# Last half chunk of an MLP by seven block products, with the last products and the final gains moved

## The chip, the cores and the metric

One Trainium2 chip, one of its cores. The metric is the device time of one execution in microseconds (us).

## The reference

A decoder block on x (256 rows, 1024 columns, float32): two attention paths, gated and added (all of it before the part that is changed), then

```
h2 = rmsnorm(x, g_mlp)
u = relu(h2 @ w_ff1)                  # 256 x 4096
x = x + (u * u) @ w_ff2               # 4096 x 1024
return rmsnorm(x, g_final)
```

## The kernel before

**Tiling.** The 4096 columns of u go in 8 chunks of 512 (`FAST` = 7 is the last), each in two halves p of 256. Every float32 operand is split into a high part, a copy in the fp32r type by ScalarE (`high_...`), and a low part, the difference by VectorE (`low_...`). `product` (L1453) multiplies by three matmuls: high by high, high by low, low by high.

For a half chunk TensorE computes u transposed (`mlp_in`, L1794: 48 matmuls of 256 columns into bank 4), ScalarE applies relu and squares it (`relu_square`, L864). The half's share of the output is then a product of 256 x 256 by 256 x 1024, taken as 2 x 2 blocks: rows 0 to 127 and 128 to 255, columns 0 to 511 and 512 to 1023 (C11, C12, C21, C22).

**Seven or eight products.** Taken plainly this is eight block products, each of three matmuls of 512 columns. For chunks 1 to 6 `mlp_products` (L1845) does seven (Winograd's form of Strassen's method), of sums of blocks: `left_sums` (VectorE) and `lefts_high`/`lefts_low` for the left side; on the right T1 and T3 by accumulating DMAs of GpSimd (`sum_blocks`, L522, on top of an extra load of SyncE into `t3_raw`, L424) and T2 and T4 by VectorE (`block_sums`). The seven results stay in seven PSUM banks and are accumulated over chunks 1 to 6.

**The end.** Chunk 7 is done plainly in both halves. TensorE's order is: the products of (6,0), `mlp_in` of (7,0), the seven products of (6,1), `mlp_in` of (7,1), then eight calls of `mlp_out_last` (L1816) of two block products each, in the order below. The last call makes C22 in two quarters of 256 columns.

```
mlp_out_last(0, 0, 0); mlp_out_last(0, 0, 1); mlp_out_last(1, 0, 0)      # t, p, n
mlp_out_last(0, 1, 0); mlp_out_last(0, 1, 1); mlp_out_last(1, 0, 1)
mlp_out_last(1, 1, 0); mlp_out_last(1, 1, 1)
```

While `mlp_in` of (7,1) runs, VectorE adds the seven banks into `xs`, the rows of x (`combine_banks`, L1324; later `combine_rows`), which also frees four of them for the plain products.

**The final norm.** As each C block is ready (`ff_done`), VectorE adds it to `xs` (`residual`, L1209, which gives `fin_res`) and, for rows 0 to 127, multiplies by the final gains (`gain`, L1411, which gives `fin_gain`). ScalarE sums the squares of the first rows (L586). VectorE adds the two sums (L1424, `fin_sum`), GpSimd takes the power -1/2 (L549, `fin_rstd`), and ScalarE scales. ScalarE's order is fixed: squares of C11 and C12, `final_act(0, 0)` (waits for `fin_gain` 1 and `fin_rstd` 1), squares of the two quarters of C22 (`ff_done` 4 and 5), `final_act(0, 1)`, `final_act(1, 0)`. For the last rows GpSimd adds the last sum (L553) and takes the power (L556); VectorE scales the quarters (L1446) and they are stored.

**Queues.** SyncE issues the weight loads in program order, each after a wait for its slot of four; ScalarE, VectorE, GpSimd and TensorE also run strictly in program order.

Of the kernel before, what the change touches and what calls it, by code (L numbers as in the profile page):

```python
# [13 lines left out]
P = 128  # L14
# [89 lines left out]
PRODUCTS = ((P1, A11, B11), (P4, A22, T4), (P7, S3, T3), (P5, S1, T1), (P2, A12, B21), (P6, S2, T2), (P3, S4, B22))  # L104
FAST = FF_CHUNKS - 1
# [13 lines left out]
def hybrid_block(nc, x, g_mix, w_in, b_gate, g_cq, w_q_up, g_ckv, w_kv_up, w_o_a, w_o_b, w_out,  # L119
# [10 lines left out]
    with ExitStack() as ctx:  # L130
# [63 lines left out]
        tail_bank = ps[:, U_BANK, P:P + QUART]  # L194
# [106 lines left out]
        last_part = sem("last_part")  # L301
# [80 lines left out]
        def _(sp):  # L382
# [33 lines left out]
            def load_w2(c, p):  # L416
# [6 lines left out]
                if 1 <= c < FAST:  # L423
                    sp.dma_start(t3_raw[:, p, :], w2_rows(c, p)[:, 0, HALF:D]).then_inc(t3_landed[p], 16)  # L424
# [27 lines left out]
            load_w2(FAST, 1)  # L452
# [14 lines left out]
        def _(pool):  # L467
# [96 lines left out]
        def _(act):  # L564
# [311 lines left out]
            def u_high(p):  # L876
                act.wait_ge(u_sq, FAST * 2 + p + 1)
                act.wait_ge(w2_used, FAST * 2 + p - 1)
                copy(left_hi_of[p][:, HALF:], left_raw[p][:, HALF:]).then_inc(uT_hi_done, 1)

            def mlp_chunk(c, first=False, last=False):
# [12 lines left out]
                if last:  # L894
                    high_last(0)
                    relu_square(c + 1, 0)
                else:
                    high_blocks(c + 1, 0)
                    high_t24(c + 1, 0)
                    relu_square(c + 1, 0)  # L900
                    high_t3(c + 1, 0)
# [53 lines left out]
        def _(dve):  # L955
# [249 lines left out]
            def residual(i, done, ready):  # L1205
# [3 lines left out]
                nc.vector.tensor_tensor(xr, ps[:, ROW_BANK[i], :], xr, ALU.add).then_inc(ready, 1)  # L1209
# [74 lines left out]
            def low_last(p):  # L1284
                s, w = (U_FF + 2 + p) % SLOTS, SLOT_W // 2
                for h in range(2):
                    dve.wait_ge(last_hi, 2 * p + h + 1)
                    nc.vector.tensor_tensor(wlo[:, s, h * w:(h + 1) * w], raw[:, s, h * w:(h + 1) * w],
                                            whi[:, s, h * w:(h + 1) * w].bitcast(F32),
                                            ALU.subtract).then_inc(last_lo, 1)  # L1290

            def left_sums(c, p):
# [9 lines left out]
                nc.vector.tensor_tensor(r[:, S4, :], r[:, S2, :], r[:, A12, :], ALU.subtract).then_inc(s_part, 1)  # L1302
# [653 lines left out]
```

## Time and profile before

| what | us |
|---|---|
| median of 3 runs (360.7 to 361.22) | 360.95 |
| the profiled execution | 361.16 |
| its span in the profile | 359.4 |
| TensorE busy | 353.2 (98%) |
| VectorE busy | 286.0 (80%) |
| ScalarE busy | 229.2 (64%) |
| GpSimd busy | 39.7 (11%) |

The profiled execution took 1.76 us more than its span. The busy time of TensorE is nearly the whole span; the granted clock is at full speed throughout. What is not TensorE's is the end, after its last matmul, which starts at 353.87 us.

### The profile page before, as it was taken

The numbers are of one execution on the slowest core, as the hardware profiler recorded it, in microseconds if no ns is written. First come the engines' busy times: TensorE is split into PE (matmuls) and PEld (weight loads), VectorE is DVE, ScalarE is ACT, GpSimd is POOL, SyncE is SP. The second block draws the span as 40 slices with busy tenths as digits, with TensorE's granted clock in tenths as the row PEclk, the third lists the DMA queues.
The fourth block names the chain that finished last, engine by engine and source line by source line (L and its number), as shares of the span: only waits on it lengthen the run. The fifth ranks groups of instructions, "written<-read, shape, count | busy, mean of one in ns | idle before, by whom it ended". The sixth has DMA issues, their size and how long they took to land.

```text
span 359.4 us, 5546 instructions
## 1 busy us (share of the span) xinstructions
PE 353.2 (98%) x2119; PEld 311.3 (87%) x2119; DVE 286.0 (80%) x402; ACT 229.2 (64%) x371; POOL 39.7 (11%) x61
## 2 busy tenths in 40 slices
PE   8999999999999999999999999999999999999994
PEld 8998889988888888888888999999999999999983
DVE  3878971789968747496687879999998898998585
ACT  4996445899675743182566567777668777665424
POOL 1242000000001000000022021111110111310001
PEclk9999999999999999999999999999999999999999
DMA  7998667491637245148076999999999999953003
GB/s 259 378 392 281 266 183 236 153 350 74 235 111 229 83 163 176 60 156 310 3 233 171 321 299 231 266 297 307 293 274 263 259 259 267 319 154 117 2 0 117
DMA packets 42197, 76.77 MB, mean 214 GB/s; under 512 B 1923, under 2 KB 19344, under 8 KB 41920
## 3 DMA queue, kind: packets, MB, share of 16 engines
q1 hardware_dynamic: 37840, 66.59, 53.8%
q0 software_dynamic: 4176, 9.64, 13.5%
q8 instruction: 13, 0.21, 0.2%
q10 hardware_dynamic: 160, 0.27, 0.2%
q14 instruction: 8, 0.07, 0.1%
HBM read 75.44 MB, written 1.05 MB: 213 GB/s over the span
## 4 chain that ended last, share of the span: by engine, by line
PE 98%; POOLq 0%; DVE 0%; issue 0%; DVEq 0%; ACT 0%; POOL 0%
PE ps L1455 30%; PE ps L1456 29%; PE ps L1457 29%; PE ps L1462 4%; PE ps L1677 2%; PE ps L1704 2%; PE ps L1562 1%; PE ps L1571 1%; PE ps L1600 0%; PE ps L1595 0%; PE ps L1605 0%; POOLq L130 0%; DVE qkT_b L1446 0%; DVEq L130 0%; ACT prob L586 0%
## 5 line engine op out<-in xcount | busy, mean ns | idle before, releaser
L566 ACT ACTIVATE whi<-raw 128x1024 fp32r<-128x1024 f32 (+3 forms) x127 | 118.8, 989 | 18.0 <-PE ps L1457 17.4
L964 DVE TENSOR_TENSOR wlo<-raw,whi 128x1024 fp32r<-128x1024 f32 (+1 forms) x56 | 64.0, 1186 | 14.9 <-ACT whi L566 14.9
L1455 PE MATMUL ps<-whi,xT_hi 128*128 128x512 f32 (+2 forms) x188 | 72.6, 386 | 0.0
L1457 PE MATMUL ps<-whi,xT_lo 128*128 128x512 f32 (+2 forms) x188 | 71.2, 379 | 0.0
L1456 PE MATMUL ps<-wlo,xT_hi 128*128 128x512 f32 (+2 forms) x188 | 71.1, 378 | 0.0
L1457 PE MATMUL ps<-xT_hi,wlo 128*128 128x256 f32 x224 | 63.4, 283 | 0.0
L1456 PE MATMUL ps<-xT_lo,whi 128*128 128x256 f32 x224 | 63.4, 283 | 0.0
L1455 PE MATMUL ps<-xT_hi,whi 128*128 128x256 f32 x224 | 63.3, 283 | 0.0
L1455 PE MATMUL ps<-whi,lat_hi 128*128 128x512 f32 (+1 forms) x124 | 47.6, 384 | 0.0
L1456 PE MATMUL ps<-wlo,lat_hi 128*128 128x512 f32 (+1 forms) x124 | 47.3, 382 | 0.0
L1457 PE MATMUL ps<-whi,lat_lo 128*128 128x512 f32 (+1 forms) x124 | 47.2, 381 | 0.0
L1456 PEld LDWEIGHTS ps<-xT_lo,whi 128*128 128x128 f32 x224 | 42.9, 192 | 0.6
L1455 PEld LDWEIGHTS ps<-xT_hi,whi 128*128 128x128 f32 x224 | 42.9, 192 | 0.5
L1457 PEld LDWEIGHTS ps<-xT_hi,wlo 128*128 128x128 f32 x224 | 42.9, 192 | 0.0
L1455 PEld LDWEIGHTS ps<-whi,xT_hi 128*128 128x128 f32 x188 | 35.3, 188 | 6.6 <-issue 0.5
L1457 PEld LDWEIGHTS ps<-whi,xT_lo 128*128 128x128 f32 x188 | 35.3, 188 | 6.4
L1456 PEld LDWEIGHTS ps<-wlo,xT_hi 128*128 128x128 f32 x188 | 35.4, 188 | 5.8
L1247 DVE TENSOR_TENSOR wlo<-raw,whi 128x1024 fp32r<-128x1024 f32 x28 | 33.9, 1219 | 0.4 <-ACT whi L566 0.4
L566 ACT ACTIVATE t_hi<-t_raw 128x1024 fp32r<-128x1024 f32 (+1 forms) x24 | 20.0, 838 | 19.2 <-DVE t_raw L1261 19.2
L1457 PEld LDWEIGHTS ps<-whi,lat_lo 128*128 128x128 f32 x124 | 23.3, 188 | 4.6
L1455 PEld LDWEIGHTS ps<-whi,lat_hi 128*128 128x128 f32 x124 | 23.4, 189 | 4.0 <-DVE ps L1430 0.2
L1456 PEld LDWEIGHTS ps<-wlo,lat_hi 128*128 128x128 f32 x124 | 23.4, 189 | 3.8
(165 smaller groups left out, 524.5 us busy)
## 6 DMA issues: line engine op xcount, KB each, us to landing
raw<-in_w_ff_dram SPq DMA_DIRECT2D x32, 1024.0 KB, 6.8
raw<-in_w_in_dram SPq DMA_DIRECT2D x14, 1024.0 KB, 6.3
raw<-in_w_out_dram SPq DMA_DIRECT2D x4, 1024.0 KB, 5.0
t_raw<-in_w_ff_dram SPq DMA_DIRECT2D x12, 256.0 KB, 7.7
raw<-in_w_ff_dram POOLq DMA_DIRECT2D x12, 256.0 KB, 4.8
t_raw<-in_w_ff_dram POOLq DMA_DIRECT2D x12, 256.0 KB, 7.1
gates<-in_b_gate_dram POOLq DMA_DIRECT2D x2, 1024.0 KB, 7.9
raw<-in_w_o_a_dram SPq DMA_DIRECT2D x2, 1024.0 KB, 5.2
```

The lines of the kernel that those rows point to most:

```text
L566: return nc.scalar.activation(dst, src, ACT.Copy, scale=scale)
L964: nc.vector.tensor_tensor(wlo[:, s, h * w:(h + 1) * w], raw[:, s, h * w:(h + 1) * w], whi[:, s, h * w:(h + 1) * w].bitcast(F32), ALU.subtr ...
L1247: nc.vector.tensor_tensor(wlo[:, s, h * w:(h + 1) * w], raw[:, s, h * w:(h + 1) * w], whi[:, s, h * w:(h + 1) * w].bitcast(F32), ALU.subtr ...
L1455: nc.tensor.matmul(dst, a_hi, b_hi, start=start, stop=False, skip_group_check=on_sums)
L1456: nc.tensor.matmul(dst, a_hi, b_lo, start=False, stop=False, skip_group_check=on_sums)
L1457: return nc.tensor.matmul(dst, a_lo, b_hi, start=False, stop=stop, skip_group_check=on_sums)
L1462: m = nc.tensor.transpose(ps[0:width, bank, b * P:(b + 1) * P], src, ident[:, :])
L1562: nc.tensor.matmul(ps[:, bank, 0:P], warm[:, :], warm[:, :], start=True, stop=True)
L1571: return nc.tensor.transpose(ps[:, bank, col:col + P], xs[:, t, k * P:(k + 1) * P], ident[:, :])
L1677: m = nc.tensor.matmul(dst, q[:, t * P:(t + 1) * P], k[:, 0:keys], start=True, stop=True)
L1704: m = nc.tensor.matmul(ps[h % 2 * 64:h % 2 * 64 + 64, O_BANK[t], h // 2 * P:(h // 2 + 1) * P], v[:, kb, h * 64:(h + 1) * 64], rows[:, g % ...
```

## The change

- The first half of chunk 7 is done by seven block products, accumulated on the same banks (`mlp_products_last`), with what they need: the extra load, `sum_blocks`, `high_blocks`, `high_t24`, `high_t3`, `block_sums`, `low_w2`, `left_sums`, `lefts_high`, `lefts_low`. Their order is P1, P6, P5, P7, P2, P3, P4.
- TensorE does `mlp_in` of (7,1) after two of the seven products of (6,1), and then the other five.
- The second half of chunk 7 stays plain. C11, C12 and C21 are accumulated straight onto the banks of P2, P3 and P4 (S4 changes its sign for that), C22 in quarters onto sums that VectorE puts into the banks of P5 and P1 (`pre_add`). Its weights go to slot 0, loaded as soon as the low part of the W1 half (7,0) is taken, and its u to the space of `xT`.
- VectorE combines the banks after the first four of the last seven products.
- GpSimd, not VectorE, multiplies rows 0 to 127 by the final gains.

The diff, cut:

```diff
+LAST_PRODUCTS = tuple(PRODUCTS[i] for i in (0, 5, 3, 2, 4, 6, 1))
+OUT_BANK = (P2, P3, P4)
+TAIL_BANK = (P5, P1)
...
 SyncE
-                if 1 <= c < FAST:
+                if c:
                     sp.dma_start(t3_raw[:, p, :], w2_rows(c, p)[:, 0, HALF:D]).then_inc(t3_landed[p], 16)
...
-            load_w2(FAST, 1)
+            sp.wait_ge(w1_lo, 4 * FAST - 2)
+            sp.dma_start(ff_slot(0).rearrange("p (f n) -> p f n", f=2),
+                         w2_rows(FAST, 1)).then_inc(raw_landed[U_FF % SLOTS], 16)
...
 GpSimd
             pool.tensor_scalar(g_fin_row, g_fin_row, ROOT_D, None, ALU.mult).then_inc(gfin_ready, 1)
+            sum_blocks(FAST, 0)
             pool.wait_ge(gfin_ready, 1)
+            for n in range(2):
+                cols = slice(n * HALF, (n + 1) * HALF)
+                pool.wait_ge(fin_res, n + 1)
+                pool.tensor_tensor(final_rows[:, 0, cols], xs[:, 0, cols], g_fin_row[:, cols],
+                                   ALU.mult).then_inc(fin_gain, 1)
             pool.wait_ge(fin_sum, 1)
             pool.tensor_tensor(rstd[:, N_FIN:N_FIN + 1], var[:, N_FIN:N_FIN + 1], neg_half[:, 0:1],
                                ALU.pow).then_inc(fin_rstd, 1)
...
 ScalarE
-            with act.Fori(2, FAST - 1) as c:
+            with act.Fori(2, FAST) as c:
                 mlp_chunk(c)
-            mlp_chunk(FAST - 1, last=True)
-            u_high(0)
-            act.wait_ge(w2_used, 2 * FAST)
+            lefts_high(FAST, 0)
+            high_last()
+            relu_square(FAST, 1)
+            u_high()
+            act.wait_ge(last_products, 1)
             copy(p1_copy, ps[:, P1, :]).then_inc(p1_read, 1)
-            high_last(1)
-            relu_square(FAST, 1)
-            u_high(1)
...
 VectorE
-            mlp_chunk(FAST - 1, last=True)
-            u_low(0)
+            left_sums(FAST, 0)
+            lefts_low(FAST, 0)
+            low_last(0)
+            low_last(1)
+            u_low()
             combine_banks()
-            low_last(1)
-            u_low(1)
-            combine_rows()
...
+            pre_add()
+            combine_rows(0)
+            combine_rows(1)
...
-            residual(0, ff_done, fin_res)
-            gain(0)
-            residual(1, ff_done, fin_res)
-            gain(1)
+            residual(0, ff_done, fin_res, OUT_BANK)
+            combine_rows(2)
+            dve.wait_ge(comb_part, 2)
+            residual(1, ff_done, fin_res, OUT_BANK)
...
 TensorE
+            def mlp_out_last(bank, t, start, width):
...
-            mlp_chunk(FAST - 1, end=True)
+            mlp_in_unit(FAST - 1, 1)
+            mlp_products(FAST - 1, 0)
+            mlp_in_unit(FAST, 0)
+            mlp_products(FAST - 1, 1, part=slice(0, 2))
             mlp_in_unit(FAST, 1)
+            mlp_products(FAST - 1, 1, part=slice(2, 7))
+            mlp_products_last()
             pe.wait_ge(last_lo, 2)
             pe.wait_ge(uT_lo_done, 3)
-            mlp_out_last(0, 0, 0)
...
-            mlp_out_last(1, 1, 1)
+            mlp_out_last(P2, 0, 0, HALF)
+            mlp_out_last(P3, 0, HALF, HALF)
+            mlp_out_last(P4, 1, 0, HALF)
+            pe.wait_ge(pre_added, 2)
+            mlp_out_last(TAIL_BANK[0], 1, HALF, QUART)
+            mlp_out_last(TAIL_BANK[1], 1, HALF + QUART, QUART)
```

`combine_banks` after: v_sum = P6 - P1 (needs `last_products` 2), q_sum = v_sum - P5 (3), C22 and C21 take P7 (4). `combine_rows(i)` adds P1 to C11, q_sum to C12, subtracts v_sum from C21, all in SBUF.

## Rows read from the trace of the kernel before

**Rows 1.** The page: busy time by engine, and the chain that ended last
```profile
PE 353.2 (98%) x2119; PEld 311.3 (87%) x2119; DVE 286.0 (80%) x402; ACT 229.2 (64%) x371; POOL 39.7 (11%) x61
...
PE 98%; POOLq 0%; DVE 0%; issue 0%; DVEq 0%; ACT 0%; POOL 0%
```

**Rows 2.** Timeline of TensorE, 325 to 360: start us, us, engine, line, what
```profile
332.44 0.40 PE L1455 MATMUL ps<-whi,lat_hi 128*128 128x512 f32 x1
...
337.23 0.28 PE L1455 MATMUL ps<-xT_hi,whi 128*128 128x256 f32 x1
...
342.99 0.40 PE L1455 MATMUL ps<-whi,lat_hi 128*128 128x512 f32 x1
...
352.54 0.30 PE L1455 MATMUL ps<-whi,lat_hi 128*128 128x256 f32 x1
...
353.87 0.28 PE L1457 MATMUL ps<-whi,lat_lo 128*128 128x256 f32 x1
```

**Rows 3.** Timeline of ScalarE, 318 to 360
```profile
332.64 0.60 ACT L867 ACTIVATE prob<-ps 128x512 f32<-128x512 f32 x1 [3.69 <-PE ps L1457]
...
350.80 0.63 ACT L586 ACTIVATE prob<-xs 128x512 f32<-128x512 f32 x1 [0.60 <-DVE xs L1209]
351.34 0.19 ACT L586 ACTIVATION_READ_ACCUMULATOR prob<-xs 128x1 f32 x1
352.53 0.72 ACT L566 ACTIVATE qkT_b<-qkT_b,rstd 128x512 f32<-128x512 f32 x1 [1.00 <-POOL rstd L549]
353.46 0.38 ACT L586 ACTIVATE prob<-ps 128x256 f32<-128x256 f32 x1 [0.21 <-PE ps L1457]
...
354.18 0.38 ACT L586 ACTIVATE prob<-ps 128x256 f32<-128x256 f32 x1 [0.24 <-PE ps L1457]
...
354.55 0.71 ACT L566 ACTIVATE qkT_b<-qkT_b,rstd 128x512 f32<-128x512 f32 x1
```

**Rows 4.** Timeline of VectorE, 318 to 360
```profile
327.69 1.22 DVE L1247 TENSOR_TENSOR wlo<-raw,whi 128x1024 fp32r<-128x1024 f32 x1
...
349.48 0.69 DVE L1415 TENSOR_TENSOR qkT_b<-xs,qkT_b 128x512 f32<-128x512 f32 x1
350.09 0.68 DVE L1209 TENSOR_TENSOR xs<-ps,xs 128x512 f32<-128x512 f32 x1
...
351.56 0.16 DVE L1424 SCALAR_TENSOR_TENSOR var<-ssq 128x1 f32<-128x1 f32 x1
...
352.74 0.69 DVE L1209 TENSOR_TENSOR xs<-ps,xs 128x512 f32<-128x512 f32 x1 [0.34 <-PE ps L1457]
...
354.27 0.68 DVE L1441 TENSOR_TENSOR qkT_b<-xs,qkT_b 128x512 f32<-128x512 f32 x1
```

**Rows 5.** Timeline of GpSimd, 300 to 360
```profile
312.69 3.33 POOL L546 TENSOR_SCALAR qkT_b<-qkT_b 128x1024 f32<-128x1024 f32 x1
351.87 0.56 POOL L549 TENSOR_TENSOR rstd<-var,neg_half 128x1 f32<-128x1 f32 x1 [35.85 <-DVE var L1424]
354.80 0.21 POOL L553 TENSOR_TENSOR var<-ssq,var 128x1 f32<-128x1 f32 x1 [2.36 <-ACT prob L586]
```

**Rows 6.** Timeline of the DMA queue of SyncE, 290 to 360
```profile
314.85 10.16 SPq L421 DMA_DIRECT2D raw<-in_w_ff_dram  x2
```

**Rows 7.** The page: DMA issues, KB each, us to landing
```profile
raw<-in_w_ff_dram SPq DMA_DIRECT2D x32, 1024.0 KB, 6.8
...
raw<-in_w_ff_dram POOLq DMA_DIRECT2D x12, 256.0 KB, 4.8
```

**Rows 8.** Timeline of VectorE, 16.5 to 20.5 and 311 to 317
```profile
18.42 2.36 DVE L964 TENSOR_TENSOR wlo<-raw,whi 128x1024 fp32r<-128x1024 f32 x2 [1.13 <-ACT whi L566]
...
313.38 1.44 DVE L1277 TENSOR_TENSOR t_lo<-t_raw,t_hi 128x512 fp32r<-128x512 f32 x1 [0.82 <-ACT t_hi L566]
```

**Rows 9.** The instructions of line 1277 (min/median/max ns)
```profile
L1277 DVE TENSOR_TENSOR t_lo<-t_raw,t_hi x12: 683/691/1435, 204.5 to 323.9; 128x512 fp32r<-128x512 f32 x12
```

**Rows 10.** Timeline of GpSimd, 0 to 310
```profile
18.62 1.11 POOL L500 TENSOR_SCALAR rstd<-rstd 128x2 f32<-128x2 f32 x1
```

More of the change, by code:

```diff
@@ L874, in lefts_high, with u_high, mlp_chunk @@
                 copy(left_hi_of[p][:, 0:LEFTS], left_raw[p][:, 0:LEFTS]).then_inc(left_hi, 1)
[L876 to L881, printed above, removed]
+            def u_high():
+                act.wait_ge(u_sq, 2 * FAST + 2)
+                copy(u_last_hi, left_raw[1][:, HALF:]).then_inc(uT_hi_done, 1)
+            def mlp_chunk(c, first=False):
                 if first:
@@ L893, in mlp_chunk @@
                 lefts_high(c, 1)
[L894 to L901, printed above, removed]
+                high_blocks(c + 1, 0)
+                high_t24(c + 1, 0)
+                relu_square(c + 1, 0)
+                high_t3(c + 1, 0)
             relu(0, 0)
@@ L1203, in _, with residual @@
             turned_low(3, mT_hi, mT_lo, 1, 1, 0.5)
-            def residual(i, done, ready):
+            def residual(i, done, ready, banks=ROW_BANK):
                 t, n = divmod(i, 2)
@@ L1208, in residual @@
                 xr = xs[:, t, n * HALF:(n + 1) * HALF]
-                nc.vector.tensor_tensor(xr, ps[:, ROW_BANK[i], :], xr, ALU.add).then_inc(ready, 1)
+                nc.vector.tensor_tensor(xr, ps[:, banks[i], :], xr, ALU.add).then_inc(ready, 1)
             def h_norm(t):
@@ new lines, in pre_add, with combine_rows @@
+            def pre_add():
+                dve.wait_ge(bank_read, 4)
+                for n in range(2):
+                    cols = slice(n * QUART, (n + 1) * QUART)
+                    nc.vector.tensor_tensor(tail[n], xs[:, 1, HALF + n * QUART:HALF + (n + 1) * QUART],
+                                            q_sum[:, cols], ALU.add).then_inc(pre_added, 1)
+            def combine_rows(i):
+                part, op = ((p1_copy, ALU.add), (q_sum, ALU.add), (v_sum, ALU.subtract))[i]
+                c = xs[:, i // 2, i % 2 * HALF:(i % 2 + 1) * HALF]
+                nc.vector.tensor_tensor(c, c, part, op).then_inc(comb_part, 1)
@@ L1357, in square, with mlp_chunk @@
                     .then_inc(u_sq, 1)
-            def mlp_chunk(c, first=False, last=False):
+            def mlp_chunk(c, first=False):
                 left_sums(c, 0)
@@ L1843, in mlp_in_unit, with block_product @@
                 mlp_in(p).then_inc(u_done, 1)
-            def mlp_products(c, p, first=False, end=False):
-                s = (U_FF + 2 + p) % SLOTS
-                pe.wait_ge(left_lo, c * 2 + p - 1)
-                pe.wait_ge(w2_lo, c * 8 + 4 * p - 4)
-                for bank, a, b in PRODUCTS:
+            def block_product(p, bank, a, b, start=False, stop=False):
+                s, a = (U_FF + 2 + p) % SLOTS, slice(a * P, (a + 1) * P)
+                if b < T3:
+                    w = slice(b * HALF, (b + 1) * HALF)
+                    b_hi, b_lo = whi[:, s, w], wlo[:, s, w]
+                elif b == T3:
+                    b_hi, b_lo = t3_hi[p], t3_lo[p]
+                else:
+                    w = slice((b - T2) * HALF, (b - T2 + 1) * HALF)
+                    b_hi, b_lo = t24_hi[p][:, w], t24_lo[p][:, w]
+                return product(ps[:, bank, :], left_hi_of[p][:, a], left_lo_of[p][:, a], b_hi, b_lo, start, stop)
@@ L1862, in mlp_products, with mlp_products_last @@
-                    m = product(ps[:, bank, :], left_hi_of[p][:, a], left_lo_of[p][:, a], b_hi, b_lo, first, end)
-                m.then_inc(w2_used, 1)
+                    m = block_product(p, bank, a, b, first)
+                if part.stop == 7:
+                    m.then_inc(w2_used, 1)
+            def mlp_products_last():
+                pe.wait_ge(left_lo, 2 * FAST - 1)
+                pe.wait_ge(w2_lo, 8 * FAST - 4)
+                for bank, a, b in LAST_PRODUCTS:
+                    m = block_product(0, bank, a, b, False, bank not in OUT_BANK)
+                    if bank not in OUT_BANK:
+                        m.then_inc(last_products, 1)
@@ L1905, in _, with mlp_chunk @@
                         m.then_inc(rows0_done, 1)
-            def mlp_chunk(c, first=False, end=False):
+            def mlp_chunk(c, first=False):
                 mlp_in_unit(c, 1)
@@ L1910, in mlp_chunk @@
                 mlp_in_unit(c + 1, 0)
[L1911 removed]
+                mlp_products(c, 1)
             mlp_chunk(1, first=True)
```

135 lines of the change are left out of this document (43 added, 92 removed).

## The prediction

> **What bounds the kernel now.** I read the page first: TensorE is busy for 353.2 us of a span of 359.4, and the chain that ended last is TensorE for 98% of it [rows 1]. So a matmul removed shortens the run, as long as nothing new makes TensorE wait and the work after its last matmul does not grow. Next the timeline of TensorE over the last two half chunks, for the pace [rows 2]: the 21 matmuls of the products of (6,1) take from 332.44 to 337.23, the 48 of `mlp_in` of (7,1) to 342.99 (0.12 each), the 42 matmuls of 512 columns behind them to 352.54, 0.2274 each. Twelve of 256 columns follow, the last starting at 353.87; with 0.12 for it they are through at 353.99. There is no gap anywhere.
>
> Then the end, on three engines. ScalarE reads the last quarter of C22 at 354.18, 0.19 after TensorE is through, and what comes behind that read is a fixed chain to 359.4. What ScalarE does before it is the point to look at [rows 3]: it computes squares of C12 from 350.80, waits for GpSimd's power, scales a row block at 352.53 (0.72), and takes the two quarters at 353.46 and 354.18. The scaling is over at 353.25, when the first quarter is not there yet. So the chain of rows 0 to 127, `residual` at 350.09, sum of squares at 351.56 [rows 4], power at 351.87 for 0.56 [rows 5], stands ahead of the last reads in ScalarE's order, and is early by little.
>
> **TensorE's part.** The first half of chunk 7 falls from eight to seven block products: 24 matmuls to 21. That is 3 x 0.2274 = 0.68 us less. The move of two products ahead of `mlp_in` of (7,1) changes the order, not the sum: by the same paces the seven last products still begin at 342.99 and end, 21 x 0.2274 later, at 347.77. Each call of C11, C12, C21 takes six matmuls, 1.364: ends at 349.13, 350.49 and 351.86. The quarters end at 352.58 and 353.30. Before, C12 was ready at 342.99 + 30 x 0.2274 = 349.81 and the last quarter at 353.99, 4.18 apart; now it is 2.81 apart.
>
> **What TensorE could wait for.** `mlp_in` of (7,1) now starts after six matmuls, at 333.83 instead of 337.23. It needs bank 4 read by the relu of (7,0), which ran from 332.64 for 0.60 [rows 3] to 333.24: 0.6 in hand; and the low part of its weights, done at 327.69 + 1.22 = 328.91 [rows 4]. The relu is now queued behind `high_blocks` and `high_t24` of (7,0): three copies of about 1 us each that begin when the products of (6,0) are over, 332.44 - 48 x 0.12 = 326.7, with VectorE's two sums in between, as in each chunk of the loop, where TensorE does not wait either. Their inputs: SyncE issues the load of (7,0) at 314.85 [rows 6]; 6.8 to landing, then GpSimd's accumulating DMA with 4.8 [rows 7] gives 326.5, against 328, when the second copy wants it. The extra `t3_raw` load and the two accumulating DMAs are those of every chunk before, with the load of (7,1) where a W1 load used to be: it waits for the low part of W1 (7,0), and so is issued some us before the 324.6 of the second load of the same row. The left sums and their high and low parts, some 4 us of VectorE and ScalarE from 333.2, must be there at 342.99; the high and low parts of the last weights and of u at 347.77. The last of these, of u, hangs on `mlp_in` of (7,1), over at 339.6 now and at 342.99 before: relu, square, copy and subtraction of 0.6 to 0.7 each end it at about 342.5. GpSimd's `sum_blocks` stands behind its multiplication of the gain row, over at 316.02, six us before the load lands. All this I cost at nothing; if the relu were late, TensorE would wait by what it is late beyond 0.6, and I keep up to 0.5 for that.
>
> VectorE's combining after the first four products: P7 is there at 345.7; C22, C21, the two pre-sums and C11 and C12 bring VectorE to about 349.3 at 0.6 to 0.7 each, just before C11 is ready (349.13 + 0.25). The quarters wait for the pre-sums, done at 348.0, needed at 351.86.
>
> **The chain of rows 0 to 127 after the change.** C12 is ready at 350.49. From the rows [rows 3 to 5]: + 0.25 to `residual`, 350.74; + 1.47 to VectorE's sum (351.56 - 350.09), 352.21; + 0.31 and 0.56 for the power, 353.08; + 0.10 to the scaling, which gives ScalarE free 0.62 later (0.72 less the overlap of about 0.1 that 350.80 and 351.34 show); + 0.37 for the first quarter (354.18 to 354.55). The last quarter's read then begins at 354.17. It began at 354.18. So even if the gains on GpSimd cost nothing, the whole 0.68 is given back here: this chain ends last in place of TensorE.
>
> **The multiplication on GpSimd.** It stands ahead of the power on GpSimd's queue, twice. No row shows GpSimd multiply two tensors of 128x512. Bounds: VectorE's 0.69 for the very same instruction [rows 4], and half of GpSimd's 3.33 for 128x1024 with one input, 1.66 [rows 5]. GpSimd's row is inflated by collisions: it began at 312.69, and a subtraction of VectorE that it met took 1.44 instead of 0.69 [rows 8, 9], so was let go at about 314.1, after 1.4 us, 0.7 for 512 columns. Two inputs should cost more than one, so I take the middle of 0.7 and 1.66, 1.2. The Trainium skill, GPSIMD Engine Reference, 3.1 Elementwise, has 4497 ns for an add of two tensors of 2048 columns; as an estimate that is about 1.15 for 512, and would take 0.1 off the sum.
>
> GpSimd and VectorE also collide. A GpSimd operation of two columns took 1.11 from 18.62 [rows 10] while VectorE ran the first of two subtractions of two SBUF tensors from 18.42, 1.18 each [rows 8]; it ended at 19.73, just behind that subtraction. In the other direction VectorE's subtraction took 0.75 too long. I take it that an instruction of VectorE with two SBUF inputs and one of GpSimd exclude each other for their length. The Trainium skill, SBUF — State Buffer, Who interferes with whom, says so: whoever starts first holds the shared interface to its end. The trace agrees in both directions, though GpSimd's 3.33 goes on behind the point where VectorE went on.
>
> So: `residual` 0 gives its rows at 350.07, but VectorE starts `combine_rows(2)`, two SBUF inputs, at 350.0, to 350.7. The first multiplication runs 350.7 to 351.9, the second to 353.1. VectorE's sum of squares (both inputs in SBUF) wants to run at 352.21 and is held to 353.1; + 0.31 + 0.56 gives the power at 353.97; + 0.10 + 0.62 + 0.37 the last quarter's read at 355.06, 0.88 late against 354.18. Behind it, GpSimd's sum for the last rows (354.80, 0.21 [rows 5]) comes 0.6 us after the first quarter's sum of squares, while VectorE's last gain product (two SBUF inputs, 354.27 for 0.68 [rows 4]) comes 0.15 after it: some 0.15 more. The rest of the end is as before. Sum: -0.68 on TensorE, given back, + 0.88 + 0.15, say + 1.0: span 360.4, the profiled execution 361.16 + 1.0 = 362.16. The median is 0.2 below the profiled execution; I say 361.9.
>
> **Rivals.**
> - *The lock does not bind, the multiplication is 1.2.* First multiplication 350.2 to 351.4, second from 351.6 to 352.8, power 353.44, read at 354.53: + 0.35, 361.3. If only the small sum escapes, + 0.55. For it: that sum is 0.16 long, and VectorE went on at 314.1 beside a GpSimd operation that lasted to 316.02. Against it: the row at 18.62.
> - *Not slower: GpSimd's multiplications are hidden.* At 0.69 the second ends at 352.3, just when the sum of squares comes, and the power is where the chain puts it anyway: 0.0, 361.0. This decides at about 0.75 each. For it: the 0.7 by the collision. Even then the run is not faster, since that chain binds; only if TensorE still ended last, with the chain of rows 0 to 127 0.6 us shorter than I add it up, would it be -0.68, 360.3.
> - *GpSimd is slow, 1.66 each, with the lock.* Multiplications end at 352.4 and 354.0; + 0.92 more than the forecast: + 1.9, 362.8.
> - *TensorE waits before `mlp_in` of (7,1)*, up to 0.5: hidden in part, since it moves C12 and all behind it: 362.4.
>
> **How the numbers follow.** A measurement of this kernel tells some 0.2% from no change, 0.72 us, so slower begins at 361.67. Chances: the forecast 0.48 (0.38 of it above 361.67, as a multiplication of 1.0 or a sum of squares that escapes brings it under), no lock 0.20 (same), hidden 0.12 (same, 0.02 of it faster), slow GpSimd 0.13, TensorE waiting 0.07 (slower). Slower 0.58, same 0.40, faster 0.02. The range leaves out the far side of the first and of the slow case: 361.0 to 362.8.
>
> **What would show it.** TensorE's last matmul starts near 353.2, 0.7 earlier, with no gap at 333.83; the two multiplications on GpSimd at 1.1 to 1.3 each, the first not before VectorE's subtraction into C21 is over; VectorE's sum of squares held up behind the second; ScalarE's last quarter read near 355, released by its own scaling and not by TensorE. It is wrong if ScalarE's last read follows TensorE by 0.2, if the multiplications take under 0.8, or if GpSimd and VectorE run side by side.

## The result, and the profile after

The changed kernel takes 361.81 us (median of 10 runs, 361.36 to 362.25), the kernel before 360.83 (10 runs, 360.62 to 361.22): 1.0027 times as long, 95% interval 1.0018 to 1.0035, or 1.0 us slower. The forecast was 361.9, in 361.0 to 362.8.

The page of the changed kernel:

```profile
span 360.3 us, 5581 instructions
...
PE 352.5 (98%) x2116; PEld 310.8 (86%) x2116; DVE 286.6 (80%) x403; ACT 230.9 (64%) x373; POOL 44.3 (12%) x65
...
PE 97%; DVE 1%; ACT 0%; issue 0%; POOL 0%; POOLq 0%; DVEq 0%; ACTq 0%
```

TensorE is busy for 0.7 us less than before [rows 1], by three matmuls fewer, and the span is 0.9 us longer. The timeline of TensorE (start us, us, engine, line, what), from the first product of (6,1), with the first matmul of the early `mlp_in` of (7,1), to the last matmul:

```profile
332.49 0.40 PE L1450 MATMUL ps<-whi,lat_hi 128*128 128x512 f32 x1
...
333.87 0.28 PE L1450 MATMUL ps<-xT_hi,whi 128*128 128x256 f32 x1
...
353.21 0.28 PE L1452 MATMUL ps<-whi,xT_lo 128*128 128x256 f32 x1
```

There is no gap: two products and then `mlp_in` follow each other, and the last matmul starts at 353.21, against 353.87 before [rows 2]. So TensorE gave what it should, 0.66. ScalarE:

```profile
332.69 0.60 ACT L879 ACTIVATE prob<-ps 128x512 f32<-128x512 f32 x1 [1.31 <-PE ps L1452]
...
353.93 0.72 ACT L578 ACTIVATE qkT_b<-qkT_b,rstd 128x512 f32<-128x512 f32 x1 [1.67 <-POOL rstd L561]
354.56 0.36 ACT L598 ACTIVATE prob<-ps 128x256 f32<-128x256 f32 x1
...
354.91 0.37 ACT L598 ACTIVATE prob<-ps 128x256 f32<-128x256 f32 x1
```

The relu of (7,0) ran as before [rows 3]. The last quarter is read at 354.91, 1.70 after the start of the last matmul; before it was 0.31. No releaser stands behind the two reads of the quarters: they follow ScalarE's own scaling at 353.93, and in the kernel before that scaling began at 352.53 [rows 3]. What held it is on VectorE and GpSimd. VectorE:

```profile
341.79 0.69 DVE L1315 TENSOR_TENSOR xT_lo<-rows,xT_hi 128x512 fp32r<-128x512 f32 x1 [1.16 <-ACT xT_hi L578]
...
348.04 1.29 DVE L1354 TENSOR_TENSOR xs<-xs,t_raw 128x512 f32<-128x512 f32 x2
...
350.08 0.68 DVE L1354 TENSOR_TENSOR xs<-xs,t_raw 128x512 f32<-128x512 f32 x1
350.80 0.69 DVE L1215 TENSOR_TENSOR xs<-ps,xs 128x512 f32<-128x512 f32 x1
352.29 0.90 DVE L1422 SCALAR_TENSOR_TENSOR var<-ssq 128x1 f32<-128x1 f32 x1 [0.79 <-ACT prob L598]
```

and GpSimd, with the line of its two gain products (min/median/max ns) behind it:

```profile
350.31 1.61 POOL L558 TENSOR_TENSOR qkT_b<-xs,qkT_b 128x512 f32<-128x512 f32 x1 [26.93 <-DVE xs L1215]
...
353.27 0.56 POOL L561 TENSOR_TENSOR rstd<-var,neg_half 128x1 f32<-128x1 f32 x1
355.52 0.40 POOL L565 TENSOR_TENSOR var<-ssq,var 128x1 f32<-128x1 f32 x1 [1.68 <-ACT prob L598]
```

```profile
L558 POOL TENSOR_TENSOR qkT_b<-xs,qkT_b x2: 1286/1446/1606, 350.3 to 351.9; 128x512 f32<-128x512 f32 x2
```

The first product waits for VectorE's subtraction into C21 (350.08 to 350.76) and takes 1.61, the second takes 1.29, to 353.16. VectorE's addition of two single columns, 0.16 before [rows 4], is held to 353.19 and takes 0.90. Only then comes the power, 353.27 against 351.87 before [rows 5].

### The profile page after: what moved, and what is told of

Its sections match the earlier page's. It is cut to its first block, busy times and chain, and to the rows that moved or that the text cites. A ratio compares the mean times of both kernels' runs of the same rounds, so it can differ in the third digit from the quotient of the medians.

```text
span 360.3 us, 5581 instructions
## 1 busy us (share of the span) xinstructions
PE 352.5 (98%) x2116; PEld 310.8 (86%) x2116; DVE 286.6 (80%) x403; ACT 230.9 (64%) x373; POOL 44.3 (12%) x65
## 4 chain that ended last, share of the span: by engine, by line
PE 97%; DVE 1%; ACT 0%; issue 0%; POOL 0%; POOLq 0%; DVEq 0%; ACTq 0%
PE ps L1450 29%; PE ps L1451 29%; PE ps L1452 29%; PE ps L1457 4%; PE ps L1672 2%; PE ps L1699 2%; PE ps L1557 1%; PE ps L1566 1%; ACT prob L598 0%; DVE xs L1215 0%; PE ps L1595 0%; DVE var L1422 0%; PE ps L1590 0%; PE ps L1600 0%; DVE xs L1354 0%
## 5 line engine op out<-in xcount | busy, mean ns | idle before, releaser
L1450 PE MATMUL ps<-whi,xT_hi 128*128 128x512 f32 (+3 forms) x198 | 76.0, 384 | 0.0
L1452 PE MATMUL ps<-whi,xT_lo 128*128 128x512 f32 (+3 forms) x198 | 74.6, 377 | 0.0
L1451 PE MATMUL ps<-wlo,xT_hi 128*128 128x512 f32 (+3 forms) x198 | 74.5, 377 | 0.0
L1450 PEld LDWEIGHTS ps<-whi,xT_hi 128*128 128x128 f32 x198 | 37.2, 188 | 6.9 <-issue 0.5
L1450 PE MATMUL ps<-whi,lat_hi 128*128 128x512 f32 (+1 forms) x110 | 42.6, 387 | 0.0
L1451 PE MATMUL ps<-wlo,lat_hi 128*128 128x512 f32 (+1 forms) x110 | 42.3, 385 | 0.0
L1452 PE MATMUL ps<-whi,lat_lo 128*128 128x512 f32 (+1 forms) x110 | 42.2, 384 | 0.0
L533 POOL DMA_DIRECT2D raw<-in_w_ff_dram x13 | 11.4, 874 | 111.1 <-DMA raw<-in_w_ff_dram 111.1
L1452 PEld LDWEIGHTS ps<-whi,lat_lo 128*128 128x128 f32 x110 | 20.7, 188 | 4.2
L1450 PEld LDWEIGHTS ps<-whi,lat_hi 128*128 128x128 f32 x110 | 20.7, 189 | 3.5
```

Source lines behind the costliest of these rows:

```text
L533: pool.dma_start(raw[:, s, HALF:2 * HALF], rows_of[:, 0, 0:HALF], accum_op=ALU.add)\
L1450: nc.tensor.matmul(dst, a_hi, b_hi, start=start, stop=False, skip_group_check=on_sums)
L1451: nc.tensor.matmul(dst, a_hi, b_lo, start=False, stop=False, skip_group_check=on_sums)
L1452: return nc.tensor.matmul(dst, a_lo, b_hi, start=False, stop=stop, skip_group_check=on_sums)
```

## The experiments

The theory is that of the prediction: the chain of rows 0 to 127 (residual of C12, squares, VectorE's sum, GpSimd's power, ScalarE's scaling) has taken TensorE's place as what ends last, which by itself gives the 0.68 us of TensorE back, and GpSimd's two products with their collisions with VectorE add some 0.9 to it. The rivals: the products are harmless and the seven products with their new order cost the time; or the products cost what they cost wherever they stand; or TensorE is still the bound underneath.

The table gives, from one profiled execution each, when TensorE's last matmul started, when ScalarE read the last quarter of C22, when VectorE began to scale the quarters and the span, and the two differences that matter. "Tail" is the span less the start of the last matmul; it is free of what differs before it between executions of one kernel (the last matmul of the kernel before started at 353.87 in one, at 354.50 in another). The last column is the recorded ratio of times to the kernel before on the same chip, with its 95% interval. Times of different chips are not compared: the median of the kernel before was 361.64 beside the first four experiments, 360.83 beside act_late, before_act_late, in_late and reordered, and 361.60 beside the other four. The ratio is not the quotient of the medians, which can be up to 0.0009 away from it.

| kernel | last matmul | last read | quarters | span | read less matmul | tail | ratio |
|---|---|---|---|---|---|---|---|
| before | 353.87 | 354.18 | 355.67 | 359.4 | 0.31 | 5.53 | 1 |
| before_again | 354.50 | 354.82 | 356.29 | 360.0 | 0.32 | 5.50 | 0.9993 (0.9985 to 1.0002) |
| before_pool | 354.41 | 354.73 | 356.20 | 359.9 | 0.32 | 5.49 | 1.0016 (1.0007 to 1.0025) |
| before_pool_again | 353.76 | 354.08 | 355.55 | 359.2 | 0.32 | 5.44 | 1.0014 (1.0002 to 1.0025) |
| before_act_late | 353.86 | 354.18 | 355.66 | 359.9 | 0.32 | 6.04 | 1.0008 (0.9998 to 1.0018) |
| changed | 353.21 | 354.91 | 356.58 | 360.3 | 1.70 | 7.09 | 1.0027 (1.0018 to 1.0035) |
| changed_again | 353.48 | 355.19 | 356.87 | 360.5 | 1.71 | 7.02 | 1.0022 (1.0012 to 1.0031) |
| dve_gains | 353.52 | 354.87 | 356.54 | 360.2 | 1.35 | 6.68 | 1.0010 (1.0000 to 1.0020) |
| pow_between | 353.21 | 354.17 | 356.40 | 360.1 | 0.96 | 6.89 | 1.0018 (1.0009 to 1.0027) |
| comb_late | 353.21 | 354.99 | 356.66 | 360.3 | 1.78 | 7.09 | 1.0026 (1.0017 to 1.0035) |
| in_late | 353.04 | 355.57 | 357.24 | 360.9 | 2.53 | 7.86 | 1.0042 (1.0029 to 1.0055) |
| act_late | 353.01 | 353.32 | 355.83 | 359.5 | 0.31 | 6.49 | 1.0008 (0.9997 to 1.0019) |
| reordered | 352.94 | 353.26 | 355.17 | 359.2 | 0.32 | 6.26 | 0.9995 (0.9982 to 1.0008) |
| one_pass | 354.46 | 354.77 | 356.35 | 360.7 | 0.31 | 6.24 | 1.0000 (0.9991 to 1.0008) |

A check on the table: for a kernel with seven products, the tail less 5.53 (the kernel before) and less TensorE's 0.68 should be its loss in us. It gives 0.88 for the changed kernel, 0.47 for dve_gains, 0.68 for pow_between, 0.88 for comb_late, 1.65 for in_late, 0.28 for act_late, 0.05 for reordered. The ratios less 1, times 361, give 0.97, 0.36, 0.65, 0.94, 1.5, 0.29, -0.18. The two agree to 0.23 or better, about the error of a comparison, so the tail accounts for the times of these.

**dve_gains.** The gains back on VectorE.

```diff
-            for n in range(2):
-                cols = slice(n * HALF, (n + 1) * HALF)
-                pool.wait_ge(fin_res, n + 1)
-                pool.tensor_tensor(final_rows[:, 0, cols], xs[:, 0, cols], g_fin_row[:, cols],
-                                   ALU.mult).then_inc(fin_gain, 1)
...
             residual(0, ff_done, fin_res, OUT_BANK)
-            combine_rows(2)
+            gain(0)
             dve.wait_ge(comb_part, 2)
             residual(1, ff_done, fin_res, OUT_BANK)
+            gain(1)
...
+            combine_rows(2)
             dve.wait_ge(comb_part, 3)
             residual(2, ff_done, fin_res, OUT_BANK)
```

> The changed kernel with both gain products of rows 0 to 127 back on VectorE, each behind its residual, and the subtraction into C21 behind the sum of squares. Theory (the chain of rows 0 to 127 ends last, and GpSimd's two products with their collisions make it 0.9 longer): the loss goes, the 0.68 of TensorE does not come; ScalarE's last quarter is read at 354.2 and the time is that of the kernel before, 360.7 to 361.1. Rival 1 (GpSimd's products are harmless, the loss is from the seven products and their order): 361.5 to 362.0, as changed. Rival 2 (without them TensorE is the bound again): 360.2.

Measured: 361.93 against 361.64 of the kernel before on this chip, 1.0010 (1.0000 to 1.0020). The larger part of the loss is gone and TensorE's 0.68 has not come, as the theory has it, but the time is 0.3 to 0.4 behind what was expected, and the last read comes 1.35 behind the last matmul where about 1.0 was expected. VectorE and GpSimd:

```profile
352.60 0.16 DVE L1425 SCALAR_TENSOR_TENSOR var<-ssq 128x1 f32<-128x1 f32 x1
352.68 0.68 DVE L1349 TENSOR_TENSOR xs<-xs,t_raw 128x512 f32<-128x512 f32 x1
...
352.91 0.88 POOL L556 TENSOR_TENSOR rstd<-var,neg_half 128x1 f32<-128x1 f32 x1 [28.71 <-DVE var L1425]
```

The power took 0.88 instead of 0.56: it met the subtraction into C21, which this edit put right there (352.68 for 0.68). Without those 0.32 us the last read would be 1.03 behind the last matmul, where the prediction's sum for products that cost nothing has 0.99 (354.17 less 353.18). That subtraction is argued: no run has this order without the collision.

**pow_between.** GpSimd's power ahead of its second product; both products stay on GpSimd.

```diff
-            for n in range(2):
-                cols = slice(n * HALF, (n + 1) * HALF)
+            def gain(n):
+                cols = slice(n * HALF, (n + 1) * HALF)
...
+            gain(0)
             pool.wait_ge(fin_sum, 1)
             pool.tensor_tensor(rstd[:, N_FIN:N_FIN + 1], var[:, N_FIN:N_FIN + 1], neg_half[:, 0:1],
                                ALU.pow).then_inc(fin_rstd, 1)
+            gain(1)
```

> The changed kernel with GpSimd's power for rows 0 to 127 ahead of its second gain product. Theory: the first product is over before VectorE's sum of squares comes, so the sum takes 0.16 and not 0.90, the power starts at 352.5 and the last quarter is read at 354.2: 360.8 to 361.2, with both products still on GpSimd. If it is the products themselves that cost (VectorE held up wherever they stand): 361.6 or more.

Measured: 362.30, 1.0018 (1.0009 to 1.0027). VectorE and GpSimd:

```profile
352.29 0.16 DVE L1425 SCALAR_TENSOR_TENSOR var<-ssq 128x1 f32<-128x1 f32 x1 [0.79 <-ACT prob L601]
...
353.09 1.79 DVE L1431 SCALAR_TENSOR_TENSOR prob<-xs 128x512 f32<-128x512 f32 x1
...
352.53 0.56 POOL L563 TENSOR_TENSOR rstd<-var,neg_half 128x1 f32<-128x1 f32 x1 [0.61 <-DVE var L1425]
353.07 1.26 POOL L558 TENSOR_TENSOR qkT_b<-xs,qkT_b 128x512 f32<-128x512 f32 x1
355.17 0.57 POOL L568 TENSOR_TENSOR var<-ssq,var 128x1 f32<-128x1 f32 x1 [0.84 <-DVE var L1436]
```

Half of the theory holds: VectorE's sum takes 0.16, the power starts at 352.53, the last quarter is read at 354.17, all as expected. But the time hardly moved, a miss; the other branch, that the products hold VectorE up wherever they stand, is the one that came nearer: the second product now starts at 353.07, in the instant in which VectorE begins the squares of C21, whose two inputs lie in SBUF. They take 1.79 instead of 0.69, and the sum for the last rows waits for them: GpSimd adds at 355.17, 0.35 before the changed kernel's 355.52. The cost of a product on GpSimd is the wait of whatever it meets; moving it moved the wait from the sum of rows 0 to 127 to that of the last rows.

**comb_late.** The subtraction into C21 behind VectorE's sum.

```diff
             residual(0, ff_done, fin_res, OUT_BANK)
-            combine_rows(2)
             dve.wait_ge(comb_part, 2)
             residual(1, ff_done, fin_res, OUT_BANK)
...
+            combine_rows(2)
             dve.wait_ge(comb_part, 3)
             residual(2, ff_done, fin_res, OUT_BANK)
```

> The changed kernel with VectorE's subtraction into C21 moved behind its sum of squares, so that the first GpSimd product meets no VectorE instruction with two SBUF inputs. Theory: that product takes 1.3 instead of 1.6, the second ends 0.3 sooner, the sum of squares is still held up: 0.3 less than the changed kernel, 361.5. Rival (no exclusion, the first product is just slower): no change, 361.8.

Measured: 362.46, 1.0026 (1.0017 to 1.0035), no gain. VectorE and GpSimd:

```profile
352.28 0.60 DVE L1421 SCALAR_TENSOR_TENSOR var<-ssq 128x1 f32<-128x1 f32 x1 [0.79 <-ACT prob L598]
352.81 0.68 DVE L1354 TENSOR_TENSOR xs<-xs,t_raw 128x512 f32<-128x512 f32 x1
...
350.31 2.56 POOL L558 TENSOR_TENSOR qkT_b<-xs,qkT_b 128x512 f32<-128x512 f32 x2 [25.63 <-DVE xs L1215]
352.96 0.95 POOL L561 TENSOR_TENSOR rstd<-var,neg_half 128x1 f32<-128x1 f32 x1
```

From the start of the first product to the end of the second it is 2.56 instead of 2.85, and VectorE's sum took 0.60 instead of 0.90, the 0.3 expected. It was lost one instruction on: the power took 0.95 instead of 0.56, behind the subtraction at 352.81. A miss in the time, but a third place where the same subtraction holds up whatever GpSimd has to do beside it.

**before_pool, before_pool_again.** The kernel before with only the gains moved to GpSimd.

```diff
+            for n in range(2):
+                cols = slice(n * HALF, (n + 1) * HALF)
+                pool.wait_ge(fin_res, n + 1)
+                pool.tensor_tensor(final_rows[:, 0, cols], xs[:, 0, cols], g_fin_row[:, cols],
+                                   ALU.mult).then_inc(fin_gain, 1)
             pool.wait_ge(fin_sum, 1)
...
             residual(0, ff_done, fin_res)
-            gain(0)
             residual(1, ff_done, fin_res)
-            gain(1)
```

> The kernel before with nothing changed but the two gain products moved to GpSimd. Theory: the quarters are ready 4.2 after C12 there, not 2.8; the products end at about 352.2, the power at 353.0, the scaling at 353.7, and the last quarter is still read when TensorE is through with it, 354.2: no change, 360.7 to 361.0. Rival (the products cost by themselves some 0.9 wherever they are): 361.7.

> The kernel before with only the two gain products on GpSimd, once more. Theory (hidden there, since the quarters come 4.2 behind C12): within 0.2 of the kernel before, and 5.5 from TensorE's last matmul to the end. Rival (the products cost something before the tail, or wherever they stand): again 0.5 or more slower.

Measured: 362.19 and 361.96, 1.0016 (1.0007 to 1.0025) and 1.0014 (1.0002 to 1.0025), some 0.5 us slower both times: a miss. GpSimd, VectorE, ScalarE and TensorE of the first:

```profile
349.71 2.55 POOL L551 TENSOR_TENSOR qkT_b<-xs,qkT_b 128x512 f32<-128x512 f32 x2 [32.89 <-DVE xs L1214]
...
351.62 0.66 DVE L1420 SCALAR_TENSOR_TENSOR var<-ssq 128x1 f32<-128x1 f32 x1 [0.79 <-ACT prob L591]
352.20 0.75 DVE L1426 TENSOR_TENSOR ps<-ps,xs 128x256 f32<-128x256 f32 x2
...
353.01 0.72 ACT L571 ACTIVATE qkT_b<-qkT_b,rstd 128x512 f32<-128x512 f32 x1 [1.43 <-POOL rstd L554]
...
354.73 0.38 ACT L591 ACTIVATE prob<-ps 128x256 f32<-128x256 f32 x1 [0.24 <-PE ps L1453]
...
352.43 0.39 PE L1453 MATMUL ps<-whi,lat_lo 128*128 128x512 f32 x1
353.01 0.38 PE L1451 MATMUL ps<-whi,lat_hi 128*128 128x256 f32 x1 [0.19 <-DVE ps L1426]
```

The part that was forecast holds: the two products end at 352.26, the scaling stands ahead of the first quarter, and the last read follows the last matmul by 0.32 as in the kernel before. The loss is elsewhere, in TensorE. VectorE's sum is held by the second product (0.66 instead of 0.16), and in this kernel `pre_added`, the sums of C22 on which TensorE's last call waits, stands behind it in VectorE's queue. So the sums come at 352.20, and the matmul that followed its predecessor by 0.23 before follows by 0.58 (352.43 to 353.01): TensorE waits 0.35, in both profiled executions, and in none of the other kernels of the table. That is most of the 0.5 to 0.6 of the ratios; the rest is within the error of a comparison. The tail is not longer (5.49 and 5.44), so the products did stay hidden there, and the rival (0.9 wherever they are) did not come either. I had asked who waits for the power and not what is queued behind the held sum. In the changed kernel the sums of C22 are made at 347.4, ahead of all this, so there this wait is not possible.

**before_again, changed_again.** Controls, nothing changed.

> Control: the kernel before, unchanged, timed as a variant against itself. All theories: a ratio of 1.0000; what it shows beside that is the error of all these comparisons. If it is off by 0.0008 or more, the small losses of the kernels that left the chain of the tail alone are no effect of their edits.

> Control: the changed kernel, unchanged, on the same chip. All theories: 0.9 to 1.0 slower than the kernel before, and 7.1 from the start of TensorE's last matmul to the end of the span, against 5.5 before.

Measured: 0.9993 (0.9985 to 1.0002) and 1.0022 (1.0012 to 1.0031). By this one control the error of a comparison is some 0.0007, or 0.25 us, and the tails of repeated kernels differ by 0.03 to 0.07.

**act_late, before_act_late.** ScalarE's first scaling of rows 0 to 127 behind the squares of the quarters, in the changed kernel and in the one before.

```diff
-            final_act(0, 0)
             act.wait_ge(ff_done, 4)
             squares(tail[0], QUART, SSQ_FIN + 3, prob[:, 3, 0:QUART])
             act.wait_ge(ff_done, 5)
             squares(tail[1], QUART, SSQ_FIN + 4, prob[:, 3, QUART:HALF])
+            final_act(0, 0)
```

> The changed kernel with one instruction of ScalarE moved: the first scaling of rows 0 to 127 behind the squares of the two quarters. Theory: ScalarE's wait for the power no longer stands ahead of the last reads; the last quarter is read at 353.5, 0.2 after TensorE; the end is then set by VectorE's sum for the last rows (not before 354.5, since it was held up by the second GpSimd product): about 0.8 less than the changed kernel, 361.0. Rival (ScalarE's order does not matter): 361.8.

> The control: the same move in the kernel before. Theory: there the last quarter is read 0.2 after TensorE anyway, so no gain: 360.7 to 361.1. Rival (the order costs in both kernels): 360.4 or less.

GpSimd of act_late:

```profile
354.60 0.57 POOL L565 TENSOR_TENSOR var<-ssq,var 128x1 f32<-128x1 f32 x1 [0.97 <-DVE var L1433]
```

The last quarter is read at 353.32, 0.31 behind the last matmul. GpSimd's addition, released by VectorE and not by ScalarE, shows that the scaling of the quarters now hangs on VectorE's sum for the last rows, held up by the second product, as expected; the addition itself took 0.57, beside VectorE's gain product. Measured: 361.33, 1.0008 (0.9997 to 1.0019), by the ratios 0.7 less than the changed kernel, where 0.8 was expected. So it was the wait for the power on ScalarE's queue through which the loss passed. In the kernel before (361.45, 1.0008, 0.9998 to 1.0018) the move leaves the last read at 354.18 and the scaling of the quarters at 355.66, where they were, as expected, but the tail grew from 5.53 to 6.04 in its profile, which no theory had. (Its ratio alone is not clear of no change.) That is the subject of the last two runs.

**in_late.** `mlp_in` of (7,1) behind all seven products of (6,1).

```diff
-            mlp_products(FAST - 1, 1, part=slice(0, 2))
-            mlp_in_unit(FAST, 1)
-            mlp_products(FAST - 1, 1, part=slice(2, 7))
+            mlp_products(FAST - 1, 1)
+            mlp_in_unit(FAST, 1)
```

> The changed kernel with the early start of mlp_in of (7,1) undone: it comes behind all seven products of (6,1). TensorE does the same matmuls. Theory: relu, square and high part of the last u now stand on ScalarE ahead of the copy of P1, and its low part on VectorE ahead of the combination, so the residual of C11 comes 0.9 to 1.0 later and all behind it: 362.6 to 362.8, with TensorE still without a gap. If the move does nothing: 361.8.

Measured: 362.52 (5 runs), 1.0042 (1.0029 to 1.0055), just below the 362.6 to 362.8 expected. VectorE's residual of C11 and ScalarE's last read:

```profile
350.15 0.69 DVE L1215 TENSOR_TENSOR xs<-ps,xs 128x512 f32<-128x512 f32 x1
...
355.57 0.37 ACT L598 ACTIVATE prob<-ps 128x256 f32<-128x256 f32 x1
```

By the last matmul's clock the residual of C11 comes 0.85 later than in the changed kernel (2.89 ahead of the last matmul instead of 3.74) and the last read 0.83 later. The early `mlp_in` is needed, for ScalarE's and VectorE's queues and not for TensorE, which has no gap in either order.

**reordered.** Seven products; the gains on VectorE where it is free; nothing of rows 0 to 127 ahead of the last reads.

```diff
-            for n in range(2):
-                cols = slice(n * HALF, (n + 1) * HALF)
-                pool.wait_ge(fin_res, n + 1)
-                pool.tensor_tensor(final_rows[:, 0, cols], xs[:, 0, cols], g_fin_row[:, cols],
-                                   ALU.mult).then_inc(fin_gain, 1)
...
             residual(1, ff_done, fin_res, OUT_BANK)
-            dve.wait_ge(ssq_done, 12)
-            nc.vector.scalar_tensor_tensor(out=var[:, N_FIN:N_FIN + 1], ...).then_inc(fin_sum, 1)
+            gain(0)
             dve.wait_ge(comb_part, 3)
             residual(2, ff_done, fin_res, OUT_BANK)
+            dve.wait_ge(ssq_done, 12)
+            nc.vector.scalar_tensor_tensor(out=var[:, N_FIN:N_FIN + 1], ...).then_inc(fin_sum, 1)
...
+            gain(1)
             nc.vector.tensor_tensor(final_rows[:, 1, 0:HALF], xs[:, 1, 0:HALF], g_fin_row[:, 0:HALF],
                                     ALU.mult).then_inc(fin_scaled, 1)
```

and on ScalarE the edit of act_late.

> The seven products kept, all gain products on VectorE in gaps (the first behind residual 1, the second behind the sum for the last rows), the sum of squares of rows 0 to 127 behind residual 2, and ScalarE's scalings behind the squares of the quarters. Theory: nothing of rows 0 to 127 stands ahead of the last reads, the last quarter is read at 353.5 and most of TensorE's 0.68 is had: 360.2 to 360.5. If something else binds: 360.8.

**one_pass.** The reordered kernel with the residual of C12 left in its PSUM bank, and

```diff
-            gain(1)
...
+            dve.wait_ge(fin_rstd, 1)
+            nc.vector.scalar_tensor_tensor(out=final_rows[:, 0, HALF:D], in0=ps[:, P3, :],
+                                           scalar=rstd[:, N_FIN:N_FIN + 1], in1=g_fin_row[:, HALF:D],
+                                           op0=ALU.mult, op1=ALU.mult).then_inc(fin_half, 1)
...
-            final_act(0, 1)
```

with SyncE's second store waiting for `fin_half`.

> The reordered kernel (seven products, all gains on VectorE, squares of the quarters first) with the second half of rows 0 to 127 finished by VectorE in one instruction from PSUM (row factor and gain at once) in place of a gain product on VectorE and a scaling on ScalarE. Theory: the two stores of rows 0 to 127 are issued closer to 354.5 and 354.8, and the last power meets fewer instructions with two SBUF inputs: the quarters are scaled at 355.0 instead of 355.2, 0.1 to 0.3 less than the kernel before. If the stores in the tail are the bound: as the reordered kernel, 0.0 to 0.1 less than before.

Measured: 360.89 and 0.9995 (0.9982 to 1.0008) for reordered, 361.71 and 1.0000 (0.9991 to 1.0008) for one_pass: the changed kernel's loss is gone, and neither beats the kernel before clear of noise. For reordered 360.2 to 360.5 was expected, a miss: something else binds. The times of one_pass cannot tell its two branches apart, since the interval holds 0.1 to 0.3 less as well as none; its trace can, below. GpSimd and VectorE of reordered:

```profile
354.25 0.89 POOL L563 TENSOR_TENSOR rstd<-var,neg_half 128x1 f32<-128x1 f32 x1
...
354.04 0.68 DVE L1440 TENSOR_TENSOR qkT_b<-xs,qkT_b 128x512 f32<-128x512 f32 x1
355.17 0.88 DVE L1445 SCALAR_TENSOR_TENSOR qkT_b<-ps,rstd,qkT_b 128x256 f32<-128x256 f32 x2 [0.45 <-POOL rstd L563]
```

Counted from the last matmul (which here starts 0.93 sooner, 0.25 more than the three matmuls account for), the last quarter is read as early as in the kernel before, but the quarters are scaled 2.23 behind it instead of 1.80: 0.34 of that went to the last power, 0.89 instead of 0.55, which met VectorE's gain product at 354.04, and 0.08 to GpSimd's addition. From there to the end it is 4.03 instead of 3.73, 0.30 more. The two together, 0.73, take back TensorE's 0.68. What the 0.30 is shows in the data moved. First the issue of the first stores, in the kernel before and in before_act_late, where nothing but ScalarE's scaling was moved:

```profile
353.28 0.36 SPq L456 DMA_DIRECT2D out_dram<-qkT_b  x1
```

```profile
355.29 0.97 SPq L456 DMA_DIRECT2D out_dram<-qkT_b  x2
```

Then, by stretches of 1 us (the stretch's length, busy time with the number of instructions of TensorE's matmuls and weight loads, VectorE, ScalarE and GpSimd, granted clock, share of the DMA engines, GB/s), the kernel before:

```profile
354.00:355.00 1.00, 0.14 (x2) 0.00 (x0) 0.92 (x4) 0.82 (x3) 0.20 (x1) 1.00 0.70 262
355.00:356.00 1.00, 0.00 (x0) 0.00 (x0) 0.33 (x1) 0.54 (x2) 0.55 (x2) 1.00 0.00 0
356.00:357.00 1.00, 0.00 (x0) 0.00 (x0) 0.54 (x2) 0.45 (x1) 0.00 (x0) 1.00 0.71 262
357.00:358.00 1.00, 0.00 (x0) 0.00 (x0) 0.00 (x0) 0.00 (x0) 0.00 (x0) 1.00 1.00 358
358.00:359.00 1.00, 0.00 (x0) 0.00 (x0) 0.00 (x0) 0.00 (x0) 0.00 (x0) 0.75 0.50 166
```

before_act_late:

```profile
356.00:357.00 1.00, 0.00 (x0) 0.00 (x0) 0.53 (x2) 0.48 (x1) 0.00 (x0) 1.00 0.86 322
357.00:358.00 1.00, 0.00 (x0) 0.00 (x0) 0.00 (x0) 0.00 (x0) 0.00 (x0) 1.00 1.04 364
358.00:359.00 1.00, 0.00 (x0) 0.00 (x0) 0.00 (x0) 0.00 (x0) 0.00 (x0) 0.75 0.97 355
```

and one_pass, in which no store is issued before 356.11:

```profile
356.00:357.00 1.00, 0.00 (x0) 0.00 (x0) 0.95 (x3) 0.67 (x2) 0.32 (x1) 1.00 0.04 14
357.00:358.00 1.00, 0.00 (x0) 0.00 (x0) 0.23 (x1) 0.13 (x1) 0.00 (x0) 1.00 1.01 373
358.00:359.00 1.00, 0.00 (x0) 0.00 (x0) 0.00 (x0) 0.00 (x0) 0.00 (x0) 0.52 1.05 373
359.00:360.00 1.00, 0.00 (x0) 0.00 (x0) 0.00 (x0) 0.00 (x0) 0.00 (x0) 0.50 0.82 289
```

In one_pass, where the last power met nothing and took 0.55, the quarters come 1.58 behind the last read, 0.33 sooner than in reordered (1.91), but the span ends 4.35 behind them, against 4.03 there and 3.73 before: all five stores, 1 MB, go out at the end, and the DMA engines are busy without a break at 373 GB/s for 2.8 us. In the kernel before the first of them had left by 355, and the second was issued at 355.3. So in one_pass what the quarters gained was lost again behind them: the stores are the bound there. ScalarE's scaling of rows 0 to 127 ahead of the last reads, which looked like the thing in the way, is what starts the first store early. That is the 0.5 of before_act_late too: the quarters are scaled when they were, the first store is issued 2.0 later, and the DMA engines have no pause before the end. In reordered they have none either (205, 369, 371 and 105 GB/s from 355 to 359).

## Why the prediction was right

- **The bound now and TensorE's part.** 0.68 less was forecast, 0.66 measured (last matmul at 353.21; the sum had 353.18). No wait in front of `mlp_in` of (7,1), which started at 333.87 (the prediction wrote 333.83; its own pace, 332.44 and six times 0.2274, gives 333.80), so the rival in which TensorE waits there falls; the last low part of u was over at 342.48 (forecast 342.5), the combination of the banks at 349.33 (349.3). The covers held as counted.
- **The chain of rows 0 to 127 ends last.** (Rival: TensorE still ends last, -0.68.) This is the step on which the sign rested: that with C12 only 2.81 ahead of the last quarter, the whole gain is given back even if GpSimd's products cost nothing. dve_gains, with its one known collision taken off, gives 1.03 from last matmul to last read against 0.99 in the sum; as it ran it has 1.35, so the 1.03 is a subtraction and no measurement.
- **The products on GpSimd.** 1.2 each, chosen between 0.7 and 1.66, measured 1.29 alone. The choice by the middle was 0.1 low; the end of the second was forecast at 353.1 and measured at 353.16, since the first got going at 350.6 and not at 350.7. Two small errors met there, which is luck.
- **The lock.** The first product was held by the subtraction (350.7 forecast, 350.6 by the trace, 351.92 less 1.29), VectorE's sum by the second, to 353.19 (353.1). The instructions that met one of the other engine took 0.90, 1.79, 0.60 and 0.66 on VectorE and 1.61, 0.88, 0.95 and 0.89 on GpSimd, each longer than alone, even with operands of one column; no instruction of VectorE with one input in PSUM was lengthened in the rows of these tails. That agrees with the rule of the Trainium skill, SBUF — State Buffer, Who interferes with whom, by which whoever starts first holds the shared interface to its end. GpSimd's 3.3 us scaling of the gain row does not fit it simply (last section). The rival without a lock falls.
- **From the sum to the last read.** The forecast had 0.31 from the moment at which VectorE's sum is let go to the power, read where nothing held it; behind the held one the power began 0.08 after its end. So the last read came at 354.91 and not 355.06: this term was 0.15 too large.
- **The last rows.** GpSimd's addition took 0.40 instead of 0.21, 0.19 for the 0.15 forecast.

The sum was + 1.0 on the span, the profile shows + 0.9, the medians + 1.0. That it comes so near is in part luck: the 0.15 too much on the way from the sum to the last read stands against 0.04 too little for the last rows. The chance of 0.58 for slower by over 0.2% was for this; the rivals of hidden products (0.0) and of slow ones (+ 1.9) are both refuted by the 1.29. The prediction calls what comes behind the last read a fixed chain. It is nearly that in the changed kernel (5.39 us instead of 5.22, 0.19 of it GpSimd's addition), but not in general: it is 5.94 in reordered and 5.7 in before_act_late, where the stores start late. This did not enter the forecast, but with the last power's collision it is why the obvious repair yields nothing.

## What to carry over

When a saturated engine is made shorter near the end of a kernel, add up again, queue by queue, the work that hangs on its earlier results: here the time between C12 and the last block shrank by 1.36 us, and the chain behind C12 had only 0.66 in hand (in the kernel before it would have let the last quarter be read at 352.53 + 0.62 + 0.37 = 353.52, and it was read at 354.18). The 0.70 that is missing is the whole gain, gone before anything else was counted. Moving an elementwise product from VectorE to GpSimd did not help here, where VectorE works on pairs of SBUF tensors: an instruction of the one that met one of the other was 0.3 to 1.1 us longer, and each edit that moved one moved the wait. Work that is finished early at the end of a kernel pays also through its store: when all five stores came late, their 1 MB took the DMA engines some 2.8 us at about 370 GB/s.

## What was not expected

- Three edits that each removed a collision (dve_gains, pow_between, comb_late) made another, of 0.3 to 1.1 us: what had been moved, or what it had been holding up, met the next instruction of the other engine.
- Five stores of 128 to 256 KB issued within 2 us ran at 373 GB/s and set the end; they took up to 2.8 us from issue to landing, against 1.8 to 2.4 in the kernel before.
- GpSimd's scaling of 128x1024 is recorded with 3.33 us in the kernel before and 3.41 in the changed one, but VectorE's subtraction that met it went on at 314.1 and at 313.5, 1.4 and 1.5 us behind the recorded starts (312.69 and 311.97), and later subtractions beside it took their usual time. In the changed kernel a subtraction of VectorE was under way from 311.39 to 312.61 and was not lengthened, so the scaling may have begun in earnest only then. Why the record goes on for 1.9 us behind the release stays open.
- The kernel before with the gains on GpSimd is slower too, through a wait of TensorE that the changed kernel does not have: the same held instruction costs through what is queued behind it, which differs from kernel to kernel.
